# Differential heads with tokens on the partitions, their norm on VectorE, and other PSUM banks for the first feed-forward chunks

## The reference, cut to what matters

```
s = jnp.einsum('mbhqd,mbhkd->mbhqk', qb, kf) * scale
s = jnp.where(dist >= 0, s + bias, NEG_INF)
p = jax.nn.softmax(s, axis=-1)
a = p[0] - lam * p[1]
...
o = rmsnorm_2(o, subln_w) * (1.0 - lam_init)
return o.reshape(B, T, H * 2 * d) @ w_out
```

## Time and profile before

| what | value |
|---|---|
| median of 3 runs | 1001.64 us (1001.53 to 1002.02) |
| the profiled execution | 1001.23 us, of which its span 999.1 us |
| PE busy | 989.2 us, 99% of the span |
| PE weight loads busy | 891.4 us, 89% |
| DVE busy | 719.1 us, 72% |
| ACT busy | 597.8 us, 60% |
| granted TensorE clock | 0.9 or more of full speed in every fortieth of the span |

### The profile page before, as it was taken

How to read it: one execution, slowest core, us unless ns; L and a number is a source line. 1 busy time by engine, 2 the same in 40 slices (tenths; PEclk the granted TensorE clock), 3 DMA queues, 4 the chain that set the end, 5 groups by cost and what they waited for, 6 DMA issues and landing times.

```text
span 999.1 us, 16659 instructions
## 1 busy us (share of the span) xinstructions
PE 989.2 (99%) x6652; PEld 891.4 (89%) x6652; DVE 719.1 (72%) x1225; ACT 597.8 (60%) x1010; POOL 0.4 (0%) x5
## 2 busy tenths in 40 slices
PE   9999999999999999999999999999999999999997
PEld 8899999998888888999999888888999899888886
DVE  5898888878888988887658665655766558565652
ACT  4778666557566666767647545554665547455452
POOL 0000000000000000000000000000000000000000
PEclk9999999999999999999999999999999999999999
DMA  9975667535656664553326555555554327555521
GB/s 369 403 250 183 260 234 288 211 128 211 211 204 227 224 234 168 211 209 127 127 87 221 204 206 203 176 184 200 216 187 142 127 106 254 194 185 175 206 82 42
DMA packets 28443, 196.72 MB, mean 197 GB/s; under 512 B 3152, under 2 KB 3664, under 8 KB 5584
## 3 DMA queue, kind: packets, MB, share of 16 engines
q1 hardware_dynamic: 28224, 195.41, 54.7%
q10 hardware_dynamic: 144, 0.26, 0.1%
HBM read 194.61 MB, written 1.05 MB: 196 GB/s over the span
## 4 chain that ended last, share of the span: by engine, by line
PE 77%; DVE 13%; ACT 6%; issue 2%; DMA 1%; SPq 0%; DVEq 0%; ACTq 0%
PE PS L1382 16%; PE PS L1269 10%; PE PS L1069 8%; PE PS L1070 7%; PE PS L1071 7%; DVE wlo L1948 7%; PE PS L1273 5%; PE PS L1222 3%; PE PS L1225 3%; PE PS L1223 3%; ACT whi L1544 2%; PE PS L1303 2%; ACT PB L1832 2%; PE PS L1304 2%; PE PS L1305 2%
## 5 line engine op out<-in xcount | busy, mean ns | idle before, releaser
L1948 DVE TENSOR_TENSOR wlo<-raw,whi 128x1024 fp32r<-128x1024 f32 x306 | 358.3, 1216 | 60.5 <-ACT whi L1544 57.9
L1544 ACT ACTIVATE whi<-raw 128x1024 fp32r<-128x1024 f32 x300 | 297.8, 1047 | 58.8 <-PE PS L1382 53.2
L1269 PE MATMUL PS<-HX,whi 128*128 128x512 f32 x736 | 230.9, 395 | 1.5 <-issue 1.5
L1273 PEld LDWEIGHTS PS<-HX,wlo 128*128 128x128 f32 x736 | 138.3, 188 | 32.3
L1069 PE MATMUL PS<-HX,whi 128*128 128x256 f32 x496 | 145.1, 292 | 0.6 <-DVE HX L1922 0.5
L1273 PE MATMUL PS<-HX,wlo 128*128 128x256 f32 x736 | 144.6, 278 | 0.0
L1070 PE MATMUL PS<-HX,whi 128*128 128x256 f32 x496 | 140.2, 283 | 0.0
L1071 PE MATMUL PS<-HX,wlo 128*128 128x256 f32 x496 | 140.1, 282 | 0.0
L1269 PEld LDWEIGHTS PS<-HX,whi 128*128 128x128 f32 x736 | 114.5, 189 | 4.2 <-issue 1.7
L1069 PEld LDWEIGHTS PS<-HX,whi 128*128 128x128 f32 x496 | 94.8, 191 | 5.9 <-issue 4.3
L1070 PEld LDWEIGHTS PS<-HX,whi 128*128 128x128 f32 x496 | 95.0, 191 | 0.2
(11 more groups left out here) (276 smaller groups left out, 1817.0 us busy)
## 6 DMA issues: line engine op xcount, KB each, us to landing
raw<-wall SPq DMA_DIRECT2D x151, 1024.0 KB, 5.1
raw<-wada SPq DMA_DIRECT2D x18, 1024.0 KB, 5.0
raw<-wall SPq DMA_DIRECT2D x8, 512.0 KB, 16.8
GA<-wada SPq DMA_DIRECT2D x2, 1024.0 KB, 21.6
GA<-alibi SPq DMA_DIRECT2D x1, 2048.0 KB, 9.4
raw<-wall SPq DMA_DIRECT2D x2, 768.0 KB, 6.2
X<-xt SPq DMA_DIRECT2D x1, 1024.0 KB, 5.0
KM<-wada SPq DMA_DIRECT2D x1, 1024.0 KB, 14.4
```

The costliest lines, as they stand in the source:

```text
L1269: e.matmul(PS[:, b + nt, :], whi[place(n)][:, at + nt * 128:at + nt * 128 + 128], HX[:, k, :, :].rearrange("p h t -> p (h t)"), start=k == ...
L1273: m = e.matmul(PS[:, b + nt, 0:T], wlo[place(n)][:, at + nt * 128:at + nt * 128 + 128], Hh[:, k, :], start=False, stop=k == 7, skip_group_ ...
L1544: e.activation(whi[place(n)][:, c], raw[i % RAW][:, c], ACT.Copy).then_inc(*up("a_whi", (n, half)))
L1948: e.tensor_tensor(wlo[place(n)][:, c], raw[i % RAW][:, c], f32(whi[place(n)][:, c]), ALU.subtract).then_inc(*up("v_wlo", (n, half)))
```

## The change

- Before the first two feed-forward chunks the turn of the banks is set to 2, so that they take banks 2 and 3. The wide chunks still begin with banks 0 and 1.
- In `values` a differential head now has the turned probabilities (PT) as the loaded operand and the values as the moving one, so that its result has tokens on the partitions: three matmuls of 128 columns in place of one of 256 and one of 128.
- `scale` keeps the reciprocals in a tile RC of its own, makes a factor LC = -lambda * sum0/sum1, and forms P0 + LC * P1 with two instructions. The missing 1/sum0 is applied when ScalarE takes the result out of PSUM, now in two instructions (one for each half of the tokens). Since ScalarE reads RC then, scale(i) first waits for the copying of head i-2, which has the same slots.
- Squares are summed on VectorE (`sub_squares`), and VectorE multiplies the results by the reciprocal roots (`sub_sums`). `sub_rows` turns these on TensorE, and `sub_out` takes the high part (ScalarE) and the low part (VectorE) out of PSUM with the gain SW.

```diff
+            st["at"] = 2
             together([("up", 0), ("up", 1)], "ffn", ev_first)
...
+                if kind == "diff":
...
+                    e.matmul(PS[:, OB, 0:128], PT[:, slot, 0:128], v[:, 0, :], start=True, stop=True)
+                    e.matmul(PS[:, OB, 128:256], PT[:, slot, 128:256], v[:, 0, :], start=True, stop=False)
+                    e.matmul(PS[:, OB, 128:256], PT[:, slot, 256:384], v[:, 1, :], start=False, stop=True).then_inc(
...
-                on.wait_ge("a_sq", ("sub", g))
                 bank(7)
                 for h in range(4):
-                    m = e.matmul(
-                        PS[:, 7, h * SUM:h * SUM + SUM], pair(SQ, 0)[:, h * 128:h * 128 + 128], ONES[:, 0:SUM],
-                        start=True, stop=True)
-                m.then_inc(*up("t_sq", ("sub", g)))
-            elif step == "sub_rows":
-                g, = a
-                on.wait_ge("v_rec", ("sub", g))
-                spread(7, 0, ST[:, 6:10], 4).then_inc(*up("t_row", ("sub", g)))
-                free[7] = ("v_nrm", ("sub", g))
+                    m = e.transpose(PS[:, 7, h * 128:h * 128 + 128], pair(TT, 0)[:, h * 128:h * 128 + 128], ID)
+                m.then_inc(*up("t_row", ("sub", g)))
+                free[7] = ("v_xlo", ("o0", g))
...
-                    e.activation(GA[:, 8 + head[1], :], PS[:, OB, 0:256], ACT.Copy).then_inc(*up("a_ev", head))
+                    for j in range(2):
+                        m = e.activation(
+                            GA[:, 8 + head[1], j * 128:j * 128 + 128], PS[:, OB, j * 128:j * 128 + 128], ACT.Identity,
+                            scale=RC[:, 2 * s0 + j:2 * s0 + j + 1])
+                    m.then_inc(*up("a_ev", head))
...
+                if head[0] == "diff":
+                    c0 = 2 * (head[1] % 2)
+                    if head[1] >= 2:
+                        on.wait_ge("a_ev", ("diff", head[1] - 2))
+                    on.wait_ge("v_lam", "lambda")
+                    e.reciprocal(RC[:, 2 * s0:2 * s1 + 2], RS[:, 2 * s0:2 * s1 + 2]).then_inc(*up("v_rs", head))
+                    on.wait_ge("v_rs", head)
+                    e.scalar_tensor_tensor(
+                        LC[:, c0:c0 + 2], RC[:, 2 * s1:2 * s1 + 2], LM[:, 4:5], RS[:, 2 * s0:2 * s0 + 2], ALU.mult,
+                        ALU.mult).then_inc(*up("v_lc", head))
+                    on.wait_ge("v_lc", head)
+                    for c, j in ((slice(0, 128), 0), (slice(128, 384), 1)):
+                        e.scalar_tensor_tensor(
+                            PB[:, s0, c], PB[:, s1, c], LC[:, c0 + j:c0 + j + 1], PB[:, s0, c],
+                            ALU.mult, ALU.add).then_inc(*up("v_p", (head, s0) if j else (head, s0, "first")))
+                    continue
...
+            elif step == "sub_squares":
+                g, = a
+                on.wait_ge("a_sq", ("sub", g))
+                if g:
+                    on.wait_ge("v_nrm", ("sub", g - 1))
+                e.tensor_reduce(
+                    ST[:, 6:10], pair(SQ, 0).rearrange("p (j t) -> p j t", j=4), mybir.AxisListType.X, ALU.add).then_inc(
+                    *up("v_sum", ("sub", g)))
             elif step == "sub_sums":
-                root_over(ST[:, 6:10], ("sub", a[0]))
+                g, = a
+                root_over(ST[:, 6:10], ("sub", g))
+                on.wait_ge("v_rec", ("sub", g))
+                is_free(tt_free, 0, 1)
+                e.tensor_tensor(
+                    pair(TT, 0).rearrange("p (j t) -> p j t", j=4), pair(GA, 8 + 2 * g).rearrange("p (j t) -> p j t", j=4),
+                    ST[:, 6:10].unsqueeze(2).to_broadcast([128, 4, 128]), ALU.mult).then_inc(*up("v_nrm", ("sub", g)))
...
-                e.scalar_tensor_tensor(
-                    pair(TT, 0), pair(GA, 8 + 2 * g), SW[:, 0:1], PS[:, 7, :], ALU.mult, ALU.mult).then_inc(
-                    *up("v_nrm", ("sub", g)))
-                low(pair(Ol, 2 * g), pair(TT, 0), pair(Oh, 2 * g), ("o0", g))
-                tt_free[0] = tt_free[1] = ("v_xlo", ("o0", g))
+                    pair(Ol, 2 * g), PS[:, 7, :], SW[:, 0:1], f32(pair(Oh, 2 * g)), ALU.mult, ALU.subtract).then_inc(
+                    *up("v_xlo", key))
```

More of the change, by code:

```diff
@@ L878, in _build @@
     RS = sb("RS", [128, 8])
+    RC = sb("RC", [128, 8])
+    LC = sb("LC", [128, 4])
     NM = sb("NM", [128, 8])
@@ L1485, in tensor @@
                 kind, i = head
[L1486 to L1489, removed]
-                    else:
[L1491 to L1499, removed]
+                if kind == "diff":
+                    slot = slots(head)[0]
+                    on.wait_ge("a_ev", (NUMBER[("qkv0", 8 + i // 2)], 0))
+                    on.wait_ge("a_t", (head, slot))
+                    bank(OB)
+                    v = V[:, :, i * 128:i * 128 + 128]
+                    e.matmul(PS[:, OB, 0:128], PT[:, slot, 0:128], v[:, 0, :], start=True, stop=True)
+                    e.matmul(PS[:, OB, 128:256], PT[:, slot, 128:256], v[:, 0, :], start=True, stop=False)
+                    e.matmul(PS[:, OB, 128:256], PT[:, slot, 256:384], v[:, 1, :], start=False, stop=True).then_inc(
+                        *up("t_o", (head, slot)))
+                    free[OB] = ("a_ev", head)
+                    continue
+                for j, slot in enumerate(slots(head)):
+                    h = 2 * i + j
+                    if kind == "fox":
+                        on.wait_ge("a_ev", (NUMBER[("in", 7 + h // 4)], 0))
+                    elif kind == "mla":
+                        on.wait_ge("a_ev", (NUMBER[("ukv", 0)], 3))
+                    else:
+                        on.wait_ge("a_ev", (NUMBER[("qkv1", 8 + h // 4)], 0))
+                    v = {"fox": VF, "mla": VM, "moba": V}[kind][:, :, h * 64:(h + 1) * 64]
+                    dst = PS[64 * j:64 * j + 64, OB, 0:256]
                     on.wait_ge("a_t", (head, slot))
@@ L1504, in tensor @@
                         *up("t_o", (head, slot)))
[L1505 to L1509, removed]
+                free[OB] = ("v_xlo", ("o1" if kind == "moba" else "heads", out_tile(head)))
+            elif step == "sub_rows":
                 g, = a
-                on.wait_ge("a_sq", ("sub", g))
+                on.wait_ge("d_small", 0)
+                on.wait_ge("v_nrm", ("sub", g))
                 bank(7)
                 for h in range(4):
-                    m = e.matmul(
-                        PS[:, 7, h * SUM:h * SUM + SUM], pair(SQ, 0)[:, h * 128:h * 128 + 128], ONES[:, 0:SUM],
-                        start=True, stop=True)
-                m.then_inc(*up("t_sq", ("sub", g)))
-            elif step == "sub_rows":
-                g, = a
-                on.wait_ge("v_rec", ("sub", g))
-                spread(7, 0, ST[:, 6:10], 4).then_inc(*up("t_row", ("sub", g)))
-                free[7] = ("v_nrm", ("sub", g))
+                    m = e.transpose(PS[:, 7, h * 128:h * 128 + 128], pair(TT, 0)[:, h * 128:h * 128 + 128], ID)
+                m.then_inc(*up("t_row", ("sub", g)))
+                free[7] = ("v_xlo", ("o0", g))
     def scalar(e):
@@ L1780, in scalar @@
                 g, = a
-                on.wait_ge("v_nrm", ("sub", g))
+                on.wait_ge("t_row", ("sub", g))
+                on.wait_ge("v_lam", "gain")
                 on.wait_ge("t_mm", heads_free(("diff", 0)))
-                e.activation(pair(Oh, 2 * g), pair(TT, 0), ACT.Copy).then_inc(*up("a_xhi", ("o0", g)))
+                e.activation(pair(Oh, 2 * g), PS[:, 7, :], ACT.Identity, scale=SW[:, 0:1]).then_inc(*up("a_xhi", ("o0", g)))
             elif step == "gates":
@@ L2288, in vector @@
+                        e.tensor_scalar(
+                            PB[:, slot, c], PB[:, slot, c], RS[:, 2 * slot + j:2 * slot + j + 1], None, ALU.mult).then_inc(
+                            *up("v_p", (head, slot) if j else (head, slot, "first")))
             elif step == "turn":
```

31 lines of the change are left out of this document (9 added, 22 removed).

## The result

| | before | after |
|---|---|---|
| median | 1001.59 us (1001.26 to 1002.02) | 1008.18 us (1007.88 to 1009.15) |
| profiled execution, span | 1001.23 us, 999.1 us | 1009.15 us, 1007.1 us |

The ratio is 1.0067, with a 95% interval of 1.0054 to 1.0080: slower, by 6.6 us, where +3.6 was forecast and +5.2 was the upper end of the range. The direction was right and the size was not. The rest of this text looks for the missing 3 us.

A forecast was written before the change was run, and what follows sets the result against it. TensorE, busy 99% of the span, was taken as the bound, except in the first feed-forward. Terms 0 + 6.3 - 0.1 - 0.9 - 1.7 = +3.6 on 1001.64 gave 1005.2 us; own range 1004.0 to 1006.6, 8-in-10 range 1002.6 to 1006.8.

The forecast's parts named there:

- The banks, 0: First wide feed-forward chunk: the 1.7 us wait goes, but VectorE's splits set the feed-forward's end; cost 0, bounds -1.7 and 0.
- the 1.7 that the forecast named as its sign: Start of the next projection, 401.5 us: TensorE would wait about 1.7 us for its input in the profile after.
- Values, no difference: Differential heads' values: three 128-column matmuls take 0.66 us, as today's two do; bounds -0.05 and +0.1 a head.
- The chain, 2.05, stops of 2.0: From values' end through ScalarE's copies and VectorE's reciprocal, LC and combinations: 2.05 us, TensorE idle 2.0; bounds 1.7 and 2.35.
- The heads, +1.7, +2.0, +1.7, +0.9: Added TensorE waits at the turns of heads 4, 5, 6 and 7, together +6.3 us.
- its rival without late waits: Copies that scale(i) waits for are long done at the differential heads: 998.9 us, or 998.3 with shorter turns; chance 0.09.
- The norm, -0.1, -0.9, -1.7: Differential heads' norm, sums taken off TensorE: gains in us at group 0, group 1, and groups 2 and 3.
- the waits cost more than their length (about 1009 us): Four 2 us stops within 35 us lower TensorE's clock behind them; chance 0.09, shared with a wait not seen.
- the first rival: Feed-forward: the banks' 1.7 us head start is kept, giving 1003.5 us; chance 0.14.

The follow-up runs named there:

- short splits: Own reciprocals with VectorE's last five feed-forward weight splits cut from 1024 to 64 columns: 997.04 us with the banks' line, 998.21 without.
- own reciprocals: Kernel after, but each differential head has its own four RC columns, so scale(i) doesn't wait for the copying: 997.90 us, ratio to before 0.9964.
- at head 5: Own reciprocals with the wait for the copying kept for head 5 alone: 1001.89 us median, in two groups.
- at head 6: Own reciprocals with the wait for the copying kept for head 6 alone: 1000.18 us median, in two groups.
- at head 4: Own reciprocals with the wait for the copying kept for head 4 alone: 1000.82 us (1000.17 to 1001.50, 11 runs).
- the heads' part alone: Kernel after without the feed-forward's bank line (st["at"] = 2): 1007.27 us, ratio to before 1.0055.
- matmuls in the stops: Kernel after with eight useless 128-column matmuls ahead of the transposes of heads 4, 5 and 6: 1005.72 us, ratio to before 1.0042.

## Why the prediction was wrong, point by point

**The banks, 0.** Right, and for the reason given (VectorE is not ready earlier): alone 1001.76 against 1001.69; with VectorE's splits short, 1.2 us of the head start are kept. Of the 1.7 the short splits can't give back all: TensorE loses 0.4 inside the end of the feed-forward, where it waits for ScalarE's copies: in the kernel with short splits it is 1.21 us from the first transpose to the next multiplication (399.54 to 400.75), in before 0.79 (400.75 to 401.54). That is a part of why the wait at the next projection was 0.9 and not the 1.7 that the forecast named as its sign. The rule of the Trainium skill to let independent groups take turns through the banks (Perfetto Trace Analysis, Matmuls) was followed by this part and brought nothing, until the engine that takes the results had time.

**Values, no difference.** Right: in the kernel with own reciprocals values(2) runs from 465.21 to turn(4) at 465.88, 0.67, where 0.66 was worked out.

**The chain, 2.05, stops of 2.0.** Right: 2.01 each, from the start of the last values matmul to the turn, a step of 0.11 included. The links were 0.72 from the copying's start to the reciprocal (0.70), 0.47 for reciprocal and LC (0.40, LC is 0.22 and not 0.17), and 0.75 for the combinations (0.75).

**The heads, +1.7, +2.0, +1.7, +0.9.** The forecast puts the four stops 6.9 us over its rival without late waits (1005.2 against 998.3). After less own reciprocals is 583.22 - 572.95 = 10.27, and without the 3.4 of the clock 6.9. Head by head, the steps of this difference are 1.9, 1.8 (3.5 with a fall), 1.9 and 1.0; by sub_rows(2) another 0.25 has come.

**The norm, -0.1, -0.9, -1.7.** Right: from before to own reciprocals -0.2 up to turn(4), -0.9 from turn(5) to sub_rows(1) and -1.8 from turn(7) to the last matmul (-1.51 to -3.34), with 0.4 at turns between. The whole is -3.3, and 997.9 us were measured for the case that the forecast put at 998.3.

**The step that failed** is a term that the sum put at nothing: TensorE's clock behind the stops. It stood only among the rivals, as "the waits cost more than their length (about 1009 us)", with a part of 0.09. The measured 1008.18 us are that rival's case. The reason for so small a part was: "The stop of 1.7 us ahead of 229.78 left the granted clock at its upper level of 2.4 GHz". The statement is true of that execution:

```profile
228.00:230.00 2.00, 0.46 (x4) 0.29 (x3) 1.97 (x6) 1.70 (x3) 0.00 (x0) 1.00 1.06 430
```

But it is one stop in one execution, and the table that it was read from could not have shown the opposite: the page gives the clock in fortieths of the span, 25 us each, in tenths, and in after, with two falls of 1.7 us, it reads 9 in every fortieth too. The runs show that a stop of 2.0 us is followed by the lower clock in some executions and not in others, at 1.7 us a time: at head 5 six of eleven by their times, at head 6 three of ten, at head 4 none that the times set apart, but probably three of eleven by the mean clock. With three such stops in the program two falls were seen in each of the traces of after and of the heads' part alone. The sum should have carried 0 to 3 times 1.7 us, so +3.6 to +8.7, and the range should have ended near 1010.

Two bounds of the prediction don't come out of its own rows. With 0.84 for the copies the chain is 2.19 and not 2.35, and the first rival's lower bound is 1004.0 - 1.7 = 1002.3 and not 1002.6. Neither would have brought in 1008.18.

The Trainium skill (TensorE: Matmul & The Clock Gate, Why this matters for your kernels) warns in that section of idle gaps of TensorE, but only of ones longer than these stops. The traces have one longer idle stretch each, at the end of the program, and there they agree: in before TensorE's last matmul starts at 993.47, and the clock is then lowered:

```profile
998.00:999.10 1.10, 0.00 (x0) 0.00 (x0) 0.00 (x0) 0.00 (x0) 0.00 (x0) 0.50 0.13 45
```

For the stops of 2.0 us the measurement decides: they are enough.

**Open:** what decides in an execution whether a stop is followed by a fall. I ran nothing that shifts the same stop in time and nothing else. Also open is why the first 56 matmuls take longer in one execution than in another (7.95 us in before, 8.49 with own reciprocals, 8.94 in after, 9.36 with one stop at head 4); this is the 0.9 us by which kernels with the same first 400 us differ ahead of 417 us, and a single trace of each can't say whether it belongs to the kernel or to the execution.

## What to carry to other kernels

When a result is taken out of PSUM later by a factor that the next-but-one task overwrites, the small tile of factors becomes a wait between engines; give each task its own columns (here 24 columns more, 10.3 us). Look first for what stands directly ahead of the released work in the waiting engine's queue, since a dependency that is "two heads old" may have been met a moment ago. And price a stop of a saturated TensorE at its length and, as a chance, at the clock behind it; work in the stop, even useless work, was cheaper than idleness.

## What the runs showed of the hardware that I had not expected

A single stop of TensorE of 2.0 us, between stretches in which it was busy all the time, can be followed by a granted clock at half (1.2 GHz in place of 2.4), which costs 1.7 us; in the two traces with three stops it fell twice, behind the first and second in one kernel and the first and third in another. The execution times of one program can then lie in two groups 1.9 to 2.4 us apart (999.5 to 1000.3 and 1001.9 to 1002.2 with one stop at head 5). With matmuls in the stops the clock didn't fall, although the work behind them started no earlier.
